# A hybrid decoder block on one core: first tiles regrouped, low weights last, inverse and gates moved by a slot

## The chip, the cores and the metric

One core of a Trainium2 chip runs one launch of the kernel. The metric is the device time in microseconds, the median of several runs. The kernel's engines are TensorE (PE, with its weight loads PEld), VectorE (DVE), ScalarE (ACT), GpSimd (POOL) and SyncE (SP), which issues most of the DMAs.

## What is computed

A residual block over x of 256 tokens by 1024 channels, in float32. From the normalised x come, through one wide projection, a gated DeltaNet branch (8 heads of 128) and a block attention branch (8 heads of 128), each with a SiLU gate; both are projected, merged by sigmoid gates, projected again, normalised and added to x.

```python
h = rms_norm(x, norm_pre_w)
proj = h @ w_in
qkv_a, z_a, beta_a, dec_a, qkv_b, z_b, gate_logits = split(proj)
qkv_a = silu(causal_depthwise_conv(qkv_a, conv_w))           # 4 taps
beta = sigmoid(beta_a)
g = -exp(dn_a_log) * softplus(dec_a + dn_dt_bias)
oa = gated_delta_rule(l2(qa), l2(ka), va, g, beta)          # inverts I + lower
ya = rms_norm(oa, dn_onorm_w) * silu(z_a)
ob = moba_attention(qb, kb, vb, rel_bias)                   # 256 tokens: one causal block, T5 bias
yb = ob * silu(z_b)
merged = gates[0] * (ya @ w_branch[0]) + gates[1] * (yb @ w_branch[1])
out = x + rms_norm(merged @ w_out, norm_post_w)
```

## The kernel before

**Numbers in two parts.** Every large product is made in three products of a rounded type: each operand is split into a high part (a cast to float32r) and a low part (the operand less its high part), and high x high, high x low and low x high are summed in PSUM. For the weights ACT makes w_hi (`split_hi`, L634) and DVE w_lo (`split_lo`, L861), for the normalised, transposed x ACT makes h_hi (L647) and DVE h_lo (L885), for eight chunks k of 128 channels.

**Tiles.** The weights come in 104 tiles of 128 x 1024 values (512 KB), loaded by SP into four slots of `raw` (`load`, L382 to L387): a pair of loads waits on `s_lo`, that is until DVE has made the low part of the tile in the slot. Tiles 0 to 15 are the keys of the eight heads (K) and the attention's values (V) in the order KVKKKVKKKKVVVVVV, tiles 16 to 27 gates, 28 to 75 six tiles for each head, 76 to 79 the last gates, 80 to 95 the branch projections (a hardware loop), 96 to 103 the output projection. One tile is 24 matmuls of 256 columns (`third`, L1236) or, for V, 12 of 512 columns (`value_third`, L1255).

**Slots of the program.** For tiles 0 to 79 each engine's program is written out by one loop over S from 0 to 239: n = S // 3 is the tile, part = S % 3 its third, and TensorE does 8 matmuls (V: 4) in a slot. Every engine works through its slots in order; what an engine does in slot S stands in `gates`, `key_front`, `key_tokens`, `similarity`, `stage_a`, `stage_u`, `stage_w` and so on, each with its own offset. ACT casts tile n + 2 in part 1 and DVE makes its low half in part 2. `stage_u` builds the second half of the triangular inverse of head g from S = U0 + 16 g, with matmuls on TensorE (L1385, L1389, L1393, L1397) and copies and 32 x 32 transposes on DVE; `stage_w` (L1406 and on) uses it from W0 + 16 g.

**The matmuls of a third** go k by k in the order w_hi h_hi, w_hi h_lo, w_lo h_hi, so that the first third already waits for w_lo:

```python
if part == 0:
    pe.wait_ge(s_hi, n + 1)
    pe.wait_ge(s_lo, lo_done(n) if not isinstance(n, int) or n != 1 else 3)
for i in range(8 * part, 8 * part + 8):
    k, which = i // 3, i % 3
```

**The start.** SP loads x in two chunks of 128 tokens. ACT and DVE sum the squares (L637, L639, L867), POOL makes the scales (L450 to L454), ACT scales chunk 0 (L642) and DVE chunk 1 (L874). TensorE runs eight warm-up matmuls (L1195), with the transpose of the small vectors (L1194) after the fifth, then transposes x, both chunks for each k (L1202). ACT casts tile 0's weights between L642 and h_hi; DVE and POOL make half of its w_lo each (L879, L458). Tile 1's w_lo is made in two halves on DVE (L879), then `wbd2`, the low part of the beta and decay weights (L891), for L1212.

**Gates and decays.** The beta and decay products run on TensorE in slot 4 (L1212), 6 and 12 (L1232 to L1234, the cumulative sums), on DVE in slots 5, 7 (L898 to L910), 11 (L916, L919) and 12 (L922 to L926), on ACT in slots 7 and 13, on POOL from L514. POOL then stores the rows of the bias and of the decays and loads them back spread over the partitions (L537 to L546): 1 MB of bias into `xin` (`climbing`), 2 x 512 KB into `th_E` (`E_all`). It copies the bias (L552) and masks the decays (L493), which ACT then takes the exponential of (L674) for `similarity` on DVE (L959). The keys are transposed on TensorE (`key_tokens`, L1316) and read by ACT (L695, L697); each waits for ACT's L697 of the key before.

## Time and profile before

| | us |
|---|---|
| median of 3 runs | 372.43 (372.27 to 372.52) |
| profiled execution | 373.05 |
| its span | 371.3 |
| PE busy | 360.4 (97%) |
| DVE busy | 270.6 (73%) |
| ACT busy | 220.4 (59%) |
| POOL busy | 62.3 (17%) |

The profiled execution is one run of its own, 0.62 us above the median. A busy share tells how long an engine had an instruction under way; matmuls overlap, and the ends of their rows are modelled, so the distance from one start to the next tells the pace. All times of rows are in us from the span's start.

### The profile page before, as it was taken

The page shows a single profiled execution, that of the slowest core. Times are in us where ns is not written, and L with a number is a line of the kernel's source. Part 1 is how long each engine was busy: PE and PEld are TensorE (multiplying, and loading weights), DVE is VectorE, ACT ScalarE, POOL GpSimd, SP SyncE. Part 2 cuts the span into 40 slices and gives each one's busy share as a digit, 9 for nine tenths or more (in the row PEclk, how much of TensorE's full clock was granted, in tenths as well). Part 3 has the DMA queues.
Part 4 walks back from the last instruction along what each step waited for, and adds up shares of the span by engine and source line. Part 5 has one row for each costly group of instructions (what it writes and reads, how often), then busy time and mean ns, then how long its engine had stood idle before and what let it go on. Part 6 is the DMA issues. An engine that isn't in the chain of part 4 may idle for free.

```text
span 371.3 us, 7660 instructions
## 1 busy us (share of the span) xinstructions
PE 360.4 (97%) x2757; PEld 344.9 (93%) x2757; DVE 270.6 (73%) x558; ACT 220.4 (59%) x500; POOL 62.3 (17%) x121
## 2 busy tenths in 40 slices
PE   8999989999999999999999999999999999999993
PEld 5889977899999999999999999999999999999882
DVE  2868886289957778878788678797786557667644
ACT  5777695344455666767757577666676643534531
POOL 3434844520050000202020201002010100000001
PEclk9999999999999999999999999999999999999998
DMA  8658935958698445554556445564446565874633
GB/s 260 178 172 248 321 117 131 286 129 219 162 234 217 127 121 151 151 148 114 140 131 184 117 114 129 146 181 116 113 124 192 140 195 146 220 221 181 229 113 113
DMA packets 99343, 62.45 MB, mean 168 GB/s; under 512 B 3652, under 2 KB 94190, under 8 KB 99310
## 3 DMA queue, kind: packets, MB, share of 16 engines
q1 hardware_dynamic: 98014, 58.59, 57.3%
q0 software_dynamic: 1296, 3.43, 3.1%
q8 instruction: 20, 0.33, 0.4%
q14 instruction: 13, 0.11, 0.1%
HBM read 60.41 MB, written 1.59 MB: 167 GB/s over the span
## 4 chain that ended last, share of the span: by engine, by line
PE 85%; ACT 4%; DVE 4%; DMA 3%; issue 2%; SPq 1%; DVEq 0%; POOL 0%; ACTq 0%; POOLq 0%
PE banks L1251 61%; PE banks L1465 6%; PE banks L1268 4%; DMA raw<-in_w_in_dram 2%; ACT th_E L674 1%; DVE w_lo L861 1%; PE banks L1350 1%; PE banks L1357 1%; ACT w_hi L634 1%; DVE acc L933 1%; ACT h_hi L647 1%; PE banks L1368 1%; DMA y<-in_dn_onorm_w_dram 1%; PE banks L1393 1%; PE banks L1195 1%
## 5 line engine op out<-in xcount | busy, mean ns | idle before, releaser
L1251 PE MATMUL banks<-h_hi,w_hi 128*128 128x256 f32 x576 | 165.6, 287 | 0.3 <-PE banks L1268 0.3
L1251 PE MATMUL banks<-h_lo,w_hi 128*128 128x256 f32 x576 | 165.4, 287 | 0.0
L1251 PE MATMUL banks<-h_hi,w_lo 128*128 128x256 f32 x576 | 165.0, 287 | 0.0
L861 DVE TENSOR_TENSOR w_lo<-raw,w_hi 128x1024 fp32r<-128x1024 f32 x102 | 124.2, 1220 | 33.1 <-ACT w_hi L634 30.2
L634 ACT CAST w_hi<-raw 128x1024 fp32r<-128x1024 f32 x104 | 107.7, 1046 | 9.3 <-PE banks L1465 4.5
L1251 PEld LDWEIGHTS banks<-h_hi,w_hi 128*128 128x128 f32 x576 | 109.9, 191 | 1.5 <-issue 1.3
L1251 PEld LDWEIGHTS banks<-h_hi,w_lo 128*128 128x128 f32 x576 | 110.0, 191 | 0.0
L1251 PEld LDWEIGHTS banks<-h_lo,w_hi 128*128 128x128 f32 x576 | 109.9, 191 | 0.0
L933 DVE SCALAR_TENSOR_TENSOR acc<-banks,vec,acc 128x255 f32<-128x255 f32 (+2 forms) x72 | 34.5, 479 | 6.2 <-ACT acc L730 3.9
L1251 PE MATMUL banks<-y_hi,w_hi 128*128 128x256 f32 x128 | 36.2, 283 | 0.0
L1251 PE MATMUL banks<-y_lo,w_hi 128*128 128x256 f32 x128 | 36.2, 283 | 0.0
L1251 PE MATMUL banks<-y_hi,w_lo 128*128 128x256 f32 x128 | 36.2, 283 | 0.0
L584 POOL TENSOR_TENSOR so<-so,rnq 128x2 f32<-128x2 f32 x8 | 4.4, 554 | 148.2 <-ACT junk L797 148.2
L1251 PEld LDWEIGHTS banks<-y_hi,w_hi 128*128 128x128 f32 x128 | 24.6, 192 | 0.0
L1251 PEld LDWEIGHTS banks<-y_lo,w_hi 128*128 128x128 f32 x128 | 24.6, 192 | 0.0
L1251 PEld LDWEIGHTS banks<-y_hi,w_lo 128*128 128x128 f32 x128 | 24.6, 192 | 0.0
L841 ACT CAST h_hi<-tacc 128x256 f32 x8 | 3.2, 406 | 28.4 <-DVE tacc L1162 28.4
L738 ACT ACTIVATE tz<-banks 128x256 f32<-128x256 f32 x16 | 6.1, 384 | 23.2 <-PE banks L1251 23.1
L730 ACT ACTIVATE acc<-banks,vec 128x256 f32<-128x256 f32 x16 | 7.6, 474 | 15.4 <-PE banks L1251 15.1
L1268 PE MATMUL banks<-w_hi,h_hi 128*128 128x512 f32 x32 | 12.8, 401 | 1.2 <-DVE w_lo L879 0.9
L1268 PE MATMUL banks<-w_lo,h_hi 128*128 128x512 f32 x32 | 12.8, 400 | 0.0
L1268 PE MATMUL banks<-w_hi,h_lo 128*128 128x512 f32 x32 | 12.8, 399 | 0.0
(235 smaller groups left out, 551.0 us busy)
## 6 DMA issues: line engine op xcount, KB each, us to landing
raw<-in_w_in_dram SPq DMA_DIRECT2D x80, 512.0 KB, 5.2
raw<-in_w_branch_dram SPq DMA_DIRECT2D x16, 512.0 KB, 4.9
raw<-in_w_out_dram SPq DMA_DIRECT2D x8, 512.0 KB, 3.7
xin<-in_x_dram SPq DMA_DIRECT2D x2, 512.0 KB, 3.9
xin<-bias_rows POOLq DMA_DIRECT2D x1, 1024.0 KB, 7.6
th_E<-g_rows POOLq DMA_DIRECT2D x2, 512.0 KB, 5.7
raw<-in_x_dram SPq DMA_DIRECT2D x2, 512.0 KB, 4.8
out_dram<-xin SPq DMA_DIRECT2D x4, 256.0 KB, 2.0
```

The source lines that it names most:

```text
L584: pool.tensor_tensor(so[:, 2:4], so[:, 0:2], rnq[:, g % 2, :], ALU.add).then_inc(s_f, 1)
L634: nc.scalar.copy(w_hi[:, t % SLOTS, :], raw[:, t % SLOTS, :]).then_inc(s_hi, 1)
L647: ac(h_hi[:, k, :], bank[k][:, 0:SEQ], ACT.Copy, scale=vec[:, R_PRE + k:R_PRE + k + 1]).then_inc(s_h_hi, 1)
L674: ac(E_all[:, h, c, :], E_all[:, h, c, :], ACT.Exp, bias=ng[:, c, h:h + 1]).then_inc(s_E, 1)
L730: ac(acc[:, t, :], ps, ACT.Copy, scale=tap(CONV - 1, 2 * t, h)).then_inc(s_tap0, 1)
L738: ac(tz[:, t - 4, :], ps, ACT.Tanh, scale=0.5).then_inc(s_tz, 1)
L861: v.tensor_tensor(w_lo[:, t % SLOTS, cols], raw[:, t % SLOTS, cols], w_hi[:, t % SLOTS, cols].bitcast(F32), ALU.subtract).then_inc(s_lo, 1)
L933: v.scalar_tensor_tensor(out=acc[:, a, i:], in0=ps[:, 0:SEQ - i], scalar=tap(CONV - 1 - i, w, h), in1=acc[:, a, i:], op0=ALU.mult, op1=ALU ...
L1195: mm(bank[6][:, 0:SEQ], acc[:, 0, 0:P], acc[:, 0, :], start=True, stop=True)
L1251: last = mm(ps, w, r, start=i == 0, stop=i == 23)
L1268: last = mm(((bE, bF), (bB, bE))[group][c], left, right, start=q == 0 and kk == 0 and which == 0, stop=q == 3 and kk == 1 and which == 2)
L1465: last = mm(bank[2 + 2 * c + e], m[:, k, P * c:P * c + P], w[:, (OUT0 + k) % SLOTS, 512 * e:512 * e + 512], start=k == 0 and m is m_hi and ...
```

## The change

- **Warm-ups:** seven in place of eight; the vector transpose stands after the sixth.
- **Norm of x:** ACT and DVE scale their squares by 1/1024 and DVE adds EPS, so POOL has one operation fewer for chunk 1 (for chunk 0 only the addition of EPS is left in it). ACT scales the second half of chunk 1, DVE the first.
- **Transposes by chunk:** all eight of chunk 0, then all eight of chunk 1 (its k = 4 to 7 wait for ACT's half).
- **Tile 0:** DVE casts w_hi, POOL makes both halves of w_lo; TensorE takes its 24 matmuls in an order written out, each with its own wait.
- **Low weights last:** in every other tile the first third is w_hi h_hi, the second w_hi h_lo, the third w_lo h_hi, and only the third waits for w_lo. V tiles likewise. In the branch tiles the wait for y_lo goes from the third part to the first.
- **Gates:** on DVE from slots 11 and 12 to 9 and 11, on TensorE from 12 to 11, on ACT from 13 to 12.
- **Inverse:** U0 from 100 to 99; the second pair of matmuls and copies at offsets 7, 8, 10, 11 in place of 6, 7, 9, 10, so these keep their slots, and what stands before them goes one slot earlier.
- **POOL:** mask_decay(0) ahead of the bias copy.

```diff
-WARM = 8
+WARM = 7
-U0, W0, UW_STRIDE = 100, 111, 16
+U0, W0, UW_STRIDE = 99, 111, 16
@@ POOL
-                if c == 1:
-                    pool.tensor_tensor(tiny[:, 1:2], tiny[:, 1:2], tiny[:, 4:5], ALU.add).then_inc(s_pre_s, 1)
-                    pool.wait_ge(s_pre_s, 1)
-                pool.tensor_scalar(tiny[:, c:c + 1], tiny[:, c:c + 1], 1.0 / D, EPS, ALU.mult, ALU.add).then_inc(s_pre_r, 1)
+                if c == 0:
+                    pool.tensor_scalar(tiny[:, 0:1], tiny[:, 0:1], 1.0, EPS, ALU.mult, ALU.add).then_inc(s_pre_r, 1)
+                else:
+                    pool.tensor_tensor(tiny[:, 1:2], tiny[:, 1:2], tiny[:, 4:5], ALU.add).then_inc(s_pre_r, 1)
...
-            pool.tensor_tensor(w_lo[:, 0, D // 2:], raw[:, 0, D // 2:], w_hi[:, 0, D // 2:].bitcast(F32),
-                               ALU.subtract).then_inc(s_lo, 1)
-            pool.wait_ge(s_lo, 2)
+            for half in range(2):
+                cols = slice(D // 2 * half, D // 2 * half + D // 2)
+                pool.tensor_tensor(w_lo[:, 0, cols], raw[:, 0, cols], w_hi[:, 0, cols].bitcast(F32),
+                                   ALU.subtract).then_inc(s_lo, 1)
+                pool.wait_ge(s_lo, half + 1)
...
             norms(0)
+            mask_decay(0)
             pool.wait_ge(s_climb, 16)
             pool.tensor_copy(bias[:], climbing[:, :, SEQ - 1::-1]).then_inc(s_bias, 1)
             pool.wait_ge(s_bias, 1)
-            mask_decay(0)
@@ ACT
             ac(xn[:, 0, :], xin[:, 0, :], ACT.Copy, scale=tiny[:, 2:3]).then_inc(s_pre_x[0], 1)
+            sa.wait_ge(s_pre_r, 5)
+            ac(xn[:, 1, D // 2:], xin[:, 1, D // 2:], ACT.Copy, scale=tiny[:, 3:4]).then_inc(s_pre_x[1], 1)
             sa.wait_ge(s_vec, 2)
-            split_hi(0, 0, 1)
...
+            sa.wait_ge(s_hi, 1)
             split_hi(1, 1, 1)
-                elif S == 13:
+                elif S == 12:
@@ DVE
-            v.tensor_scalar(xn[:, 1, :], xin[:, 1, :], tiny[:, 3:4], None, ALU.mult).then_inc(s_pre_x[1], 1)
+            v.tensor_scalar(xn[:, 1, 0:D // 2], xin[:, 1, 0:D // 2], tiny[:, 3:4], None, ALU.mult).then_inc(s_pre_x1a, 1)
+            ve.wait_ge(s_raw[0], 16)
+            v.tensor_copy(w_hi[:, 0, :], raw[:, 0, :]).then_inc(s_hi, 1)
...
-            first_lo(0, 0, s_lo)
-                elif S == 11:
+                elif S == 9:
-                elif S == 12:
+                elif S == 11:
-                elif s == 7:
+                elif s == 8:
-                elif s == 10:
+                elif s == 11:
@@ PE
-                if n == WARM - 3:
+                if n == WARM - 1:
...
-                pe.wait_ge(s_pre_x[c], 1)
-            for k in range(KT):
-                if k == 7:
-                    pe.wait_ge(s_vec, 1)
-                for c in range(NC):
+                pe.wait_ge((s_pre_x[0], s_pre_x1a)[c], 1)
+                for k in range(KT):
+                    if k == 7 and c == 0:
+                        pe.wait_ge(s_vec, 1)
+                    elif k == 4 and c == 1:
+                        pe.wait_ge(s_pre_x[1], 1)
                     last = tp(bank[k][:, P * c:P * c + P], xn[:, c, P * k:P * k + P], ident)
-                last.then_inc(s_hT, 1)
+                    if c == 1:
+                        last.then_inc(s_hT, 1)
-                elif S == 12:
+                elif S == 11:
+            def first_tile():
+                ps = bank[0][:, 0:SEQ]
+                order = ("hh0 hh1 lh0 hh2 lh1 hh3 lh2 hl0 hh4 lh3 hl1 hh5 lh4 hl2 hh6 lh5 hl3 hh7 lh6 lh7 "
+                         "hl4 hl5 hl6 hl7").split()
+                pe.wait_ge(s_hi, 1)
+                pe.wait_ge(s_h_lo, 1)
+                for i, which in enumerate(order):
+                    k = int(which[2])
+                    if which[0] == "l":
+                        pe.wait_ge(s_h_lo, k + 1)
+                    else:
+                        pe.wait_ge(s_h_hi, k + 1)
+                    if which[1] == "l":
+                        pe.wait_ge(s_lo, 1 + k // 4)
...
                 if part == 0:
                     pe.wait_ge(s_hi, n + 1)
-                    pe.wait_ge(s_lo, lo_done(n) if not isinstance(n, int) or n != 1 else 3)
-                elif isinstance(n, int) and n == 1:
-                    pe.wait_ge(s_lo, 4)
-                for i in range(8 * part, 8 * part + 8):
-                    k, which = i // 3, i % 3
...
+                elif part == 2:
+                    pe.wait_ge(s_lo, lo_done(n))
+                for k in range(KT):
+                    w = (w_lo if part == 2 else w_hi)[:, slot, P * k:P * k + P]
+                    r = (right_lo if part == 1 else right_hi)[:, k, :]
+                    last = mm(ps, w, r, start=part == 0 and k == 0, stop=part == 2 and k == KT - 1)
...
-                elif s == 6:
+                elif s == 7:
-                elif s == 9:
+                elif s == 10:
...
-                        if part == 2 and t < 2:
+                        if part == 0 and t < 2:
                             pe.wait_ge((s_ylo_b, s_ylo_a)[t], HEADS)
```

## Rows read from the trace of the kernel before

**Rows 1.** Waits of TensorE, whole span: engine, line, releaser: total us, times, longest.

```profile
PE banks L1316 <- ACT k_all L697: 1.0, 2, 0.6
...
PE banks L1406 <- DVE sub L1100: 0.4, 1, 0.4
```

**Rows 2.** Timeline 0 to 22 us: start, duration, engine, line, operation [idle before <-releaser].

```profile
1.19 4.63 PE L1195 MATMUL banks<-acc 128*128 128x256 f32 x10 [1.19 <-DVE acc L864]
...
6.66 2.78 PE L1195 MATMUL banks<-acc 128*128 128x256 f32 x6
6.74 1.15 ACT L642 ACTIVATE xin<-xin,tiny 128x1024 f32<-128x1024 f32 x1 [0.40 <-POOL tiny L454]
...
7.92 0.75 DVE L874 TENSOR_SCALAR xin<-xin,tiny 128x1024 f32<-128x1024 f32 x1 [0.47 <-POOL tiny L454]
...
9.10 1.71 POOL L458 TENSOR_TENSOR w_lo<-raw,w_hi 128x512 fp32r<-128x512 f32 x1 [1.22 <-ACT w_hi L634]
...
9.90 3.09 ACT L647 ACTIVATE h_hi<-banks,vec 128x256 fp32r<-128x256 f32 x8 [0.94 <-PE banks L1202]
10.41 3.26 DVE L885 SCALAR_TENSOR_TENSOR h_lo<-banks,vec,h_hi 128x256 fp32r<-128x256 f32 x8 [0.72 <-ACT h_hi L647]
...
12.83 1.09 ACT L634 CAST w_hi<-raw 128x1024 fp32r<-128x1024 f32 x1
...
13.97 1.09 ACT L634 CAST w_hi<-raw 128x1024 fp32r<-128x1024 f32 x1
14.03 1.29 DVE L879 TENSOR_TENSOR w_lo<-raw,w_hi 128x512 fp32r<-128x512 f32 x2 [0.36 <-ACT w_hi L634]
...
15.24 0.28 DVE L891 TENSOR_TENSOR wbd<-wbd 128x128 fp32r<-128x128 f32 x1
...
15.47 0.47 PE L1268 MATMUL banks<-w_hi,h_hi 128*128 128x512 f32 x1 [0.89 <-DVE w_lo L879]
...
16.47 0.28 PE L1212 MATMUL banks<-h_hi,wbd 128*32 128x256 f32 x1
```

**Rows 3.** Timeline of TensorE, the transposes of x, in two windows.

```profile
9.44 1.02 PE L1202 MATMUL banks<-cst,xin 128*128 128x128 f32 x4
...
10.29 1.36 PE L1202 MATMUL banks<-cst,xin 128*128 128x128 f32 x11
```

**Rows 4.** Timeline 20 to 30 us, all engines.

```profile
20.79 0.19 DVE L904 TENSOR_TENSOR bd<-banks,bd_lo 128x32 f32<-128x32 f32 x1
...
24.35 1.22 DVE L861 TENSOR_TENSOR w_lo<-raw,w_hi 128x1024 fp32r<-128x1024 f32 x1 [2.50 <-PE banks L1251]
...
27.39 1.23 DVE L861 TENSOR_TENSOR w_lo<-raw,w_hi 128x1024 fp32r<-128x1024 f32 x1
...
27.52 0.60 PE L1232 MATMUL banks<-cst,tab 128*8 128x128 f32 x4
...
28.65 0.99 SPq L387 DMA_DIRECT2D raw<-in_w_in_dram  x2
28.71 0.41 DVE L922 COPY grow<-banks 8x256 f32<-8x256 f32 x1
...
29.96 0.95 POOL L542 DMA_DIRECT2D xin<-bias_rows  x1
```

**Rows 5.** The chain of waits, 35 to 50 us: start, us, what.

```profile
35.29 7.63 DMA raw<-in_w_in_dram
```

**Rows 6.** Timeline of ACT, 42 to 45 us.

```profile
42.95 1.05 ACT L634 CAST w_hi<-raw 128x1024 fp32r<-128x1024 f32 x1 [1.39 <-DMA raw<-in_w_in_dram]
```

**Rows 7.** Busy time by window: window, PE, PEld, DVE, ACT, POOL, PEclk, DMA share, GB/s.

```profile
30.00:32.00 2.00, 2.00 (x17) 1.91 (x16) 1.93 (x4) 1.49 (x3) 0.92 (x1) 1.00 0.98 272
```

**Rows 8.** Timeline of TensorE around L1393 of head 0 and of head 7.

```profile
128.35 0.49 PE L1393 MATMUL banks<-T_all,lac 128*128 128x128 f32 x2
...
271.46 0.49 PE L1393 MATMUL banks<-T_all,lac 128*128 128x128 f32 x2 [0.20 <-DVE T_all L1091]
```

**Rows 9.** Timeline of POOL, 107 to 110 us.

```profile
107.28 2.60 POOL L572 DMA_DIRECT2D T_all<-t_blocks  x4 [3.72 <-DMA t_blocks<-sub]
```

More of the change, by code:

```diff
@@ L1234, in gates, with third @@
                     mm(bA[:, 16:32], ones, tab[:, 9:11, :], start=True, stop=True).then_inc(s_gc_p, 1)
-            def third(n, t, part, right_hi, right_lo, first_tile=False, out_bank=None):
+            def first_tile():
[12 more added lines that the diff above has]
+                        pe.wait_ge(s_lo, 1 + k // 4)
+                    last = mm(ps, (w_lo if which[1] == "l" else w_hi)[:, 0, P * k:P * k + P],
+                              (h_lo if which[0] == "l" else h_hi)[:, k, :], start=i == 0, stop=i == 23)
+                last.then_inc(s_tile, 1)
+            def third(n, t, part, right_hi, right_lo, out_bank=None):
                 ps = bank[t % 2 if out_bank is None else out_bank][:, 0:SEQ]
@@ L1260, in value_third @@
                     pe.wait_ge(s_hi, n + 1)
+                elif part == 2:
                     pe.wait_ge(s_lo, lo_done(n))
-                for m in range(4 * part, 4 * part + 4):
-                    kk, c, which = m // 6, m // 3 % 2, m % 3
-                    if group == 1 and q == 0 and m == 3:
-                        pe.wait_ge(s_vtok, 1)
-                    left = (h_lo if which == 2 else h_hi)[:, 2 * q + kk, P * c:P * c + P]
-                    right = (w_lo if which == 1 else w_hi)[:, slot, 512 * kk:512 * kk + 512]
-                    last = mm(((bE, bF), (bB, bE))[group][c], left, right, start=q == 0 and kk == 0 and which == 0,
-                              stop=q == 3 and kk == 1 and which == 2)
-                    if q == 3 and kk == 1 and which == 2 and c == 0:
-                        last.then_inc(s_vg_p, 1)
+                for kk in range(2):
+                    for c in range(NC):
+                        if group == 1 and q == 0 and part == 0 and kk == 0 and c == 1:
+                            pe.wait_ge(s_vtok, 1)
+                        left = (h_lo if part == 1 else h_hi)[:, 2 * q + kk, P * c:P * c + P]
+                        right = (w_lo if part == 2 else w_hi)[:, slot, 512 * kk:512 * kk + 512]
+                        last = mm(((bE, bF), (bB, bE))[group][c], left, right, start=q == 0 and kk == 0 and part == 0,
+                                  stop=q == 3 and kk == 1 and part == 2)
+                        if q == 3 and kk == 1 and part == 2 and c == 0:
+                            last.then_inc(s_vg_p, 1)
                 if part == 2:
@@ L1448, in _ @@
                         bank_free(n)
-                    third(n, n, part, h_hi, h_lo, first_tile=n == 0,
-                          out_bank=K_TILES.index(n) % 2 if n < GATES_A else None)
+                    third(n, n, part, h_hi, h_lo, out_bank=K_TILES.index(n) % 2 if n < GATES_A else None)
             with pe.Fori(0, KT // 2) as i:
```

18 lines of the change are left out of this document (8 added, 10 removed).

## The prediction

> **What bounds the kernel now.** The profiled execution took 373.05 us (span 371.3); the median of three runs is 372.43, so 0.62 comes off every sum against the profile. I read the page's busy shares first (PE 97% busy), which say only that TensorE sets the time. The second view is what TensorE waited for [rows 1]. It lists hardly 5 us in 371, nearly all in the start; behind it stand 1.0 us in two waits for ACT's L697, 0.4 at L1406, and 0.2 at L1393 [rows 8]. In between, a 256-column matmul starts every 0.12 us, and nothing in the change alters their number. So the time is a start, a fixed queue of matmuls, a few holes and a tail. The change can win only in the start and the holes, and a gain at the start counts only if no hole behind it grows.
>
> The third view is the start in order of time [rows 2]. Eight warm-up matmuls are sixteen records: ten from 1.19, six from 6.66, each 0.43 us. The last holds the queue until 9.23, although x's second chunk is scaled at 7.92 + 0.75 = 8.67. Then ACT makes h_hi (8 in 3.09, from 9.90) and DVE h_lo (8 in 3.26, from 10.41), and ACT casts tile 1 at 12.83. DVE subtracts its low half in two pieces from 14.03 to 15.32, and only then, at 15.47, does TensorE begin tile 1; the beta and decay product (L1212) begins at 16.47. I take that row as the meter of the start.
>
> The fourth view is 20 to 30 us [rows 4]: the decay sums reach DVE at 20.79, then ACT's gates and its cast of tile 4, DVE's low half at 24.35, at 27.39 that of tile 5, which frees the slots for the loads at 28.65. From there [rows 5 to 7]: DVE frees tile 6's slot at 35.29, the load of tile 10 takes 7.63 us because POOL's bias and decay loads share the DMA engines, ACT waits 1.39 us for it and casts at 42.95. ACT is then busy without a break until both of TensorE's waits for L697.
>
> **The start, worked out.** POOL drops one small operation, an estimated 0.3 us, on the way to the second scale, whose user starts at 7.92: it is there at about 7.6. DVE scales half a chunk, less than the 0.75 of the whole, ACT the other half after its first chunk (6.74 + 1.15 = 7.89) by 8.6. Both lie beside the transposes of chunk 0. Six warm-ups ahead of the vector transpose end at 1.19 + 12 x 0.43 = 6.35, where that transpose went anyway (just before 6.66); the seventh ends at 7.52. TensorE idles until 7.9, loads weights and starts the transposes at about 8.1. What follows depends on their pace. The trace has two [rows 3]: 0.21 us start to start until 10.3, and 0.11 after it. The granted clock reads 1.00 (the 2.4 GHz level) in both stretches, so that column doesn't show it; I read the slower cadence as the 1.2 GHz level. TensorE had been stopped from about 5.8 to 6.4 for the vector rows, and was busy from there until the pace doubled. The change fills most of that stop (the queue runs from 1.19 to 7.5 almost unbroken) and opens one of 0.5 us later. At the fast pace chunk 0 takes 0.9, the first h_hi can start at about 9.3 (0.6 earlier); at the slow pace 1.7 and 10.35 (0.45 later). I take the fast one, as the long unbroken stretch now comes first.
>
> DVE's cast of tile 0 has no row of its own. Its bounds are a one-input operation of the same size, 0.75, and the two-input L861, 1.22 [rows 2, 4]; either ends by 9.4, before the first h_lo. POOL then does two halves of 1.71 (before: one), ending near 12.8; the new order asks for the second only behind the last h_lo (about 12.9), so it costs 0, or up to 0.5 if POOL runs slower beside DVE. POOL's memsets move back by as much, into time in which it waits for the gates. ACT no longer casts tile 0 before h_hi, but that cast was hidden.
>
> So h_hi ends near 12.4, ACT's cast of tile 1 near 13.3, DVE's two halves 13.4 to 14.7, L891 14.9. Tile 1 may begin with its high weights alone and isn't the limit; L1212 waits for L891 and starts at 15.1 in place of 16.47: **1.35 earlier** for TensorE. DVE can't follow fully. ACT's cast of tile 2 at 13.97 follows that of tile 1 and its load, which the change doesn't move; I take it as fixed, so DVE's chain through conv comes only 0.4 earlier there, and the decay sums (20.79) by 0.9. Gates on DVE moved from slot 11 to 9 then run behind w_lo of tile 4 (24.35 - 0.9 + 1.22 = 24.7) and end at 25.3. TensorE's gate matmuls, now in slot 11, start at 25.4, before one slot (0.96) later at 27.52. 27.52 - 0.96 - 25.4 = **1.2 is what TensorE carries past the gates**; the hole of about 0.3 ahead of L1232 stays, only smaller or larger with the rest.
>
> **The loads.** The copy of grow (28.71) comes about 2.0 earlier, so POOL's store and its bias load (29.96) go at 27.8. But the gate copies (grow's 0.41 and three small ones, an estimated 0.75 us on DVE) now stand ahead of w_lo of tile 5, which therefore ends at 28.65, as before, and releases the loads of tiles 8 and 9 at the same time as before. The DMA engines begin the saturated stretch [rows 7] about 1.1 earlier with the same bytes; tile 7's low half and the load of tile 10 (35.29) come 0.8 earlier. I put tile 10's landing 1.05 earlier (bounds: 0 and 2.4, where ACT waits no more). ACT is wanted there 1.2 earlier and so waits 1.5 in place of 1.39, and the two holes at L1316 keep their size. **Carried past slot 34: 1.05.** mask_decay(0) ahead of the bias copy is worth nothing here, for ACT reaches the first decay later than the mask even now; the bias copy is 1.5 us later against its use, of which DVE's first similarity has several to spare.
>
> **The rest.** Low weights last: w_lo is due two slots later. After tile 1 no row of TensorE waits for it, so 0. The value tiles signal chunk 0 two matmuls later and ask for the copied bank two earlier, each 0.24 [rows 2]: 0, at worst 0.5 once. The branch tiles ask for all of y_lo a part or two earlier, but its last instruction stands ahead of them in program order: 0. The inverse: its first three steps go one slot earlier, the third and fourth matmul stay. L1393 now has two slots behind DVE's corner transposes. Holes ahead of it [rows 8]: 0.2 idle once, and the stretched 0.49 us rows; start to start I count 0.3 and 0.35 over the usual 0.12. I take 0.55 (bounds 0.2 and 0.7). T_all's load was issued by 109.9 [rows 9], some 10 us ahead of the new first step. L1406's 0.4 stays.
>
> Sum: 1.05 + 0.55 = 1.6. 373.05 - 1.6 = 371.45 profiled; **372.43 - 1.6 = 370.8**, alone 370.2 to 371.4.
>
> **Rivals.** (a) Tile 10 lands early enough, since the decay rows are stored and loaded before the stretch is full: the holes of 1.0 go too, and all of 1.2 is kept: 1.2 + 1.0 to 1.3 + 0.55, about 369.5. For: the store of g_rows now comes before the saturated stretch, so the decay loads are queued early. Against: the same bytes are moved before tile 10's. (b) The slow pace lasts until 10.3: h_hi is 0.45 later, L1212 still 0.5 earlier through tile 1's relaxed wait, DVE's chain not at all; 0.3 + 0.55, so 371.6. (c) The earlier decay loads crowd out tiles 8 to 10, nothing passes slot 34: 0.55, 371.9. (d) The other sign: the slow pace outlasts the transposes by far. Then tile 0's 24 matmuls cost 0.24 each from about 11.0, end at 16.7 in place of 14.4, and push the conv chain that starts from tile 0 by 1.8; 1.5 reach the sums at 20.79, less 0.55 is 373.4. It decides where the pace doubles: past 16 us slower, before 13 no loss. For it speaks the new 0.5 us stop, and that transposes follow it instead of warm-ups; against, that the pace doubled in the middle of transposes before. The Trainium skill (TensorE: Matmul & The Clock Gate, Part 4: PE-mode transpose) says that transposes don't count as busy for the clock; by that rule (d) or (b) is what happens, though the trace, with its doubling among transposes, neither proves nor refutes it. The skill's page DMA: Bandwidth & Descriptors (Queues, rings and completion order) has each DMA engine alternate between queues by packet; by it (c) gains, as POOL's loads get their share whenever they are queued, and the 7.63 us of tile 10's load agrees. (e) Nothing measurable: all is hidden behind tile 10's load.
>
> **How the numbers follow.** Forecast 0.46, (a) 0.16, (b) 0.12, (c) and (e) 0.18, (d) 0.08. A change of 0.2%, 0.75 us, is about what a measurement of this kernel can tell. Faster by more (under 371.68): the forecast, (a), most of (b) and a quarter of the rest, 0.75; within 0.2% 0.17; slower (over 373.18) 0.08. The range leaves out (d) and the far half of (a): 369.5 to 372.2.
>
> **What would show it.** Right: transposes 0.11 apart from about 8.1, h_hi from 9.3, L1212 near 15.1, its gate matmuls near 25.4, the bias load at 27.8, tile 10's cast near 41.9 with a wait of over 1 us, both waits on L697 still there, none on L1393. Wrong: transposes 0.21 apart (b, d); no waits on L697 (a); tile 10 cast after 42.5 (c); new waits in TensorE's list behind 60 us, which I don't have.

## The result and the profile after

The changed kernel takes **374.95 us** (median of four runs, 374.65 to 375.86) beside 372.35 for the kernel before on the same chip: ratio 1.0074, interval 1.0055 to 1.0093. It is slower by 2.6 us, where the forecast was 370.8. The profiled execution took 374.69 us (span 372.9); TensorE's last matmul starts at 366.83 in place of 365.18.

I read it as I read the kernel before: first what TensorE waited for (engine, line, releaser: total us, times, longest), of the changed kernel. L1340 is the old L1316 and L1430 the old L1406, so these lines answer [rows 1].

```profile
PE banks L1340 <- ACT k_all L701: 4.3, 2, 3.9
...
PE banks L1430 <- DVE sub L1105: 0.4, 1, 0.4
```

One wait of 3.9 us is new, and the wait on the inverse (L1393 in [rows 8]) is gone. The start, as a timeline (start, duration, engine, line, operation), of the changed kernel; it answers [rows 2 to 4]:

```profile
7.77 1.97 PE L1208 MATMUL banks<-cst,xin 128*128 128x128 f32 x16 [0.46 <-ACT xin L644]
8.09 0.69 DVE L880 CAST w_hi<-raw 128x1024 fp32r<-128x1024 f32 x1
8.92 2.64 POOL L460 TENSOR_TENSOR w_lo<-raw,w_hi 128x512 fp32r<-128x512 f32 x2 [1.43 <-DVE w_hi L880]
9.08 3.02 ACT L650 ACTIVATE h_hi<-banks,vec 128x256 fp32r<-128x256 f32 x8 [0.75 <-PE banks L1208]
14.70 0.31 PE L1219 MATMUL banks<-h_hi,wbd 128*32 128x256 f32 x1
...
19.19 0.19 DVE L909 TENSOR_TENSOR bd<-banks,bd_lo 128x32 f32<-128x32 f32 x1
...
24.71 0.60 PE L1239 MATMUL banks<-cst,tab 128*8 128x128 f32 x4
```

Everything here came as forecast or earlier: transposes 0.12 us apart, DVE's cast of tile 0 0.69 (bounds 0.75 and 1.22), POOL's halves 1.32 each (taken as 1.71), the first h_hi at 9.1, the meter of the start at 14.70 (forecast 15.1, before 16.47), the decay sums at 19.19, the gate matmuls at 24.7. The loss comes next. The timeline from 26 to 42 us, changed kernel:

```profile
26.58 1.22 DVE L865 TENSOR_TENSOR w_lo<-raw,w_hi 128x1024 fp32r<-128x1024 f32 x1
26.62 0.55 POOL L541 DMA_DIRECT2D g_rows<-grow  x1 [2.64 <-DVE grow L927]
27.16 0.95 POOL L544 DMA_DIRECT2D xin<-bias_rows  x1
...
27.83 1.03 SPq L387 DMA_DIRECT2D raw<-in_w_in_dram  x2
28.55 1.08 POOL L548 DMA_DIRECT2D th_E<-g_rows  x2 [0.43 <-DMA g_rows<-grow]
...
39.05 1.04 ACT L636 CAST w_hi<-raw 128x1024 fp32r<-128x1024 f32 x1 [5.32 <-DMA raw<-in_w_in_dram]
...
41.06 0.66 PE L1340 MATMUL banks<-cst,kT_all 128*128 128x128 f32 x2 [3.91 <-ACT k_all L701]
```

The loads of tiles 8 and 9 are issued at 27.83, earlier than before (28.65), but now POOL's store and bias load stand ahead of them and its decay loads 0.7 us behind. The summaries of the transfers (KB each, median us from issue to landing) for 28 to 31 us of before and 27 to 29 of after:

```profile
raw<-in_w_in_dram SPq DMA_DIRECT2D x2, 512.0 KB, 4.8
xin<-bias_rows POOLq DMA_DIRECT2D x1, 1024.0 KB, 7.6
```

```profile
xin<-bias_rows POOLq DMA_DIRECT2D x1, 1024.0 KB, 7.3
raw<-in_w_in_dram SPq DMA_DIRECT2D x2, 512.0 KB, 11.9
th_E<-g_rows POOLq DMA_DIRECT2D x1, 512.0 KB, 7.4
```

A weight tile that took 4.8 us takes 11.9. ACT, which never waited for tiles 8 and 9 before, waits 5.32, and TensorE behind it 3.91. And the wait has an echo: busy time by window (window, its length, PE busy, PEld, DVE, ACT, POOL, granted clock, DMA share, GB/s) of the changed kernel.

```profile
38.00:41.00 3.00, 0.00 (x0) 0.00 (x0) 0.88 (x1) 1.92 (x7) 2.30 (x2) 0.98 1.11 347
41.00:42.00 1.00, 0.94 (x5) 0.97 (x6) 0.96 (x3) 1.00 (x2) 0.00 (x0) 0.50 0.71 260
42.00:43.00 1.00, 1.00 (x6) 1.00 (x6) 0.96 (x3) 0.23 (x2) 0.00 (x0) 0.50 0.17 49
43.00:44.00 1.00, 1.00 (x6) 1.00 (x6) 1.00 (x1) 0.97 (x6) 0.00 (x0) 0.50 0.00 0
...
45.00:46.00 1.00, 1.00 (x11) 1.00 (x10) 0.60 (x2) 1.00 (x2) 0.84 (x3) 1.00 0.68 96
```

After TensorE has stood still for nearly 4 us its granted clock is 0.50 (the 1.2 GHz level) for about 3 us: 6 matmuls in a microsecond in place of 11. The stretch from the key transposes to the end of the slot's matmuls takes 3.60 us (41.06 to 44.65), and 2.13 in the kernel before, so the clock costs 1.47. For the balance I compare the same matmul in both profiled runs, before and after:

```profile
38.66 0.38 PE L1316 MATMUL banks<-cst,kT_all 128*128 128x128 f32 x2
54.22 0.41 PE L1316 MATMUL banks<-cst,kT_all 128*128 128x128 f32 x2 [0.37 <-ACT k_all L697]
```

```profile
36.03 1.12 PE L1274 MATMUL banks<-h_hi,w_hi 128*128 128x256 f32 x8
57.24 0.41 PE L1340 MATMUL banks<-cst,kT_all 128*128 128x128 f32 x2 [0.37 <-ACT k_all L701]
```

The last of the eight matmuls ahead of the wait starts at 36.87, and at the usual 0.12 the key transposes would have come at 36.99: 1.67 earlier than the 38.66 of before. They come at 41.06, so the hole is 4.07, start to start. With the clock's 1.47 TensorE is then 3.87 later than before. By 57.24 it is 3.02 later, since 0.85 of waits is gone, most of it the old hole at slot 30, and the part with the inverse gains 1.37 up to the last matmul: 4.07 + 1.47 - 1.67 - 0.85 - 1.37 = +1.65, the distance between the last matmuls.

**Why the tile loads are so slow: the packets.** The trace counts packets, bytes and the share of the 16 DMA engines by queue; q1 is SP's, q0 POOL's. First before, 31:32 (tiles 8 and 9 alone) and 34:35 (POOL's loads alone), then after, 34:35, both at once:

```profile
q1 hardware_dynamic: 687, 0.34, 115.0%
...
q0 software_dynamic: 82, 0.34, 99.1%
```

```profile
q0 software_dynamic: 99, 0.36, 87.1%
q1 hardware_dynamic: 99, 0.05, 16.7%
```

0.34 MB in 687 packets is 0.5 KB in each, the row of 128 numbers of a weight tile; 0.34 MB in 82 is 4.1 KB. Once both queues have been moving packets for a microsecond, as many leave one as the other: 54 and 54 at 31:32, 56 and 57, 97 and 100, 99 and 99, 93 and 93 in the microseconds behind it. One for one is then one byte in nine for the weight tiles. While POOL's 2 MB pass (about 512 packets), tiles 8 and 9 get 512 packets of 0.5 KB, a quarter of their 1 MB; the rest takes 2.3 us at 0.33 MB/us, and with POOL's last packets at 36.4 this makes 38.7: ACT's cast starts at 39.05. The Trainium skill (DMA: Bandwidth & Descriptors, Queues, rings and completion order) has each DMA engine take a packet from each queue in turn, and from 31 us on this trace agrees; what the prediction left out is that the turn is blind to size.

**The first microseconds are no turn.** The queue that comes second moves nothing for a while. First after, 29:30 (the tiles issued at 27.83 have no packet until 30.2), then before, 37:38 (tile 10, issued at 35.29, has none until just before 39):

```profile
q0 software_dynamic: 52, 0.21, 84.8%
```

```profile
q0 software_dynamic: 97, 0.36, 99.3%
```

In both microseconds SP's queue has no line. So two things make the 11.9 us: the order of issue (2.4 us without a packet, where tiles 8 and 9 of before had their first 1.0 us behind their issue) and then the packets one for one. What holds the second queue back, no run shows.

The kernel before avoids it by an accident of its order. There the store of g_rows goes behind tiles 8 and 9 and lands 4.6 us later, so the decay loads can't be issued before 34.3; and the bias load, issued at 29.96, 1.3 us behind the tiles, moves nothing until about 33.

### The profile page after: what moved, and what is told of

Read it like the earlier page. It is cut to its first block, busy times and chain, and to the rows that moved or that the text cites. A ratio compares the mean times of both kernels' runs of the same rounds, so it can differ in the third digit from the quotient of the medians.

```text
span 372.9 us, 7655 instructions
## 1 busy us (share of the span) xinstructions
PE 359.8 (96%) x2755; PEld 344.8 (92%) x2755; DVE 268.9 (72%) x558; ACT 219.2 (59%) x500; POOL 62.4 (17%) x121
## 4 chain that ended last, share of the span: by engine, by line
PE 88%; DMA 4%; ACT 4%; DVE 2%; issue 1%; POOL 1%; DVEq 0%; POOLq 0%; ACTq 0%
PE banks L1274 63%; PE banks L1491 6%; PE banks L1292 4%; DMA raw<-in_w_in_dram 3%; ACT th_E L678 1%; PE banks L1374 1%; PE banks L1259 1%; PE banks L1381 1%; PE banks L1392 1%; DMA xin<-in_x_dram 1%; PE banks L1430 1%; PE banks L1219 1%; ACT junk L699 1%; PE banks L1433 1%; PE banks L1437 0%
## 5 line engine op out<-in xcount | busy, mean ns | idle before, releaser
L1274 PE MATMUL banks<-h_lo,w_hi 128*128 128x256 f32 x568 | 83.1, 289 | 0.0
L1274 PE MATMUL banks<-h_hi,w_lo 128*128 128x256 f32 x568 | 82.8, 289 | 0.0
L1274 PE MATMUL banks<-h_hi,w_hi 128*128 128x256 f32 x568 | 82.1, 287 | 0.3 <-PE banks L1292 0.3
L1274 PEld LDWEIGHTS banks<-h_hi,w_hi 128*128 128x128 f32 x568 | 72.7, 191 | 1.4 <-issue 1.4
L1274 PEld LDWEIGHTS banks<-h_lo,w_hi 128*128 128x128 f32 x568 | 73.5, 193 | 0.0
L1274 PEld LDWEIGHTS banks<-h_hi,w_lo 128*128 128x128 f32 x568 | 73.3, 192 | 0.0
L1274 PE MATMUL banks<-y_hi,w_hi 128*128 128x256 f32 x128 | 18.0, 283 | 0.0
L1274 PE MATMUL banks<-y_lo,w_hi 128*128 128x256 f32 x128 | 18.0, 283 | 0.0
L1274 PE MATMUL banks<-y_hi,w_lo 128*128 128x256 f32 x128 | 18.0, 283 | 0.0
L1274 PEld LDWEIGHTS banks<-y_hi,w_hi 128*128 128x128 f32 x128 | 16.5, 192 | 0.0
```

Source lines behind the costliest of these rows:

```text
L1274: last = mm(ps, w, r, start=part == 0 and k == 0, stop=part == 2 and k == KT - 1)
```

## The experiments

All times are medians, each set beside runs of the kernel before on the same chip (372.28 to 372.44). "Version 3" is the kernel of experiment 3, and so on. "Hole" is start to start on TensorE over the usual pace; at slot 30 it is read across the key transposes (from the matmul ahead of them to the one behind, less 0.29), which gives 0.87 for the kernel before. Rows and holes are of one profiled execution of each version.

**1. The gates' slots put back in the change**, all else as changed (the four are ACT's, DVE's two and TensorE's).

```diff
-                elif S == 12:
+                elif S == 13:
...
-                elif S == 9:
+                elif S == 11:
...
-                elif S == 11:
+                elif S == 12:
...
-                elif S == 11:
+                elif S == 12:
```

> The changed kernel with the gate slots as before (DVE 11 and 12, TensorE 12, ACT 13), all else changed. Theory Q (queue order): in the changed kernel POOL's bias load went out at 27.2 us and its decay loads at 28.6, beside the loads of tiles 8 and 9 at 27.8, which then took 11.2 and 12.6 us in place of 4.1 and 5.4. With the gate copies behind the low half of tile 5 again, that low half ends near 26 us and the loads of tiles 8 and 9 are queued 1 us or more ahead of the bias load: they take 4 to 6 us, the hole of 3.8 us ahead of the key transposes and the slow stretch after it are gone, and the time is 370.3 to 371.3. Rival S (the earlier start by itself outruns the loads): the hole stays at 3 us or more, time 374 to 375. Rival M (the mask ahead of the bias copy holds up ACT): no change either, 374 to 375.

Measured: 371.6, ratio 0.9974 (0.9964 to 0.9984). Tiles 8 and 9 are issued at 27.14, the bias load at 28.46, the decay loads at 33.33; the tiles take 5.0 us, the hole of 4 us is gone. A hole of 1.67 at 43.8 is new; experiment 14 explains it.

**2. The gates' slots alone moved in the kernel before** (the same four numbers the other way).

> The kernel before with the gate slots alone moved (DVE 9 and 11, TensorE 11, ACT 12). Theory Q: the bias load comes before the loads of tiles 8 and 9 here too, these take over 9 us, a hole of 2 to 4 us opens ahead of the key transposes at tile 8, and the time is 374 to 377, slower than before. Rival S and rival M: no such hole, for neither the start nor the mask has moved; 372.0 to 372.6.

Measured: 376.94, ratio 1.013 (1.0113 to 1.0147): +4.7 us, with tiles 8 and 9 at 11.7 us and a hole of 3.94 at 41.7. This one part costs more than the change loses; the other parts win some of it back.

**3. The bias load behind the tiles.** In the change POOL waits for conv's eighth tap.

```diff
+            pool.wait_ge(s_tap, 8)
             pool.dma_start(climbing, bass.AP(bias_rows.tensor, 0, ...)).then_inc(s_climb, 16)
```

> The changed kernel with one wait more on POOL: the bias load waits until DVE has done the second conv tap of the third key tile (about 29 us), so it and the decay loads are queued about 1.2 us behind the loads of tiles 8 and 9; the gate slots stay as changed. Theory Q: tiles 8 and 9 land in 4 to 7 us, no hole there, 370.3 to 371.8 (tile 10's load, queued behind the decay rows, may still leave the holes of about 1 us further on). Rival S and M: the hole stays, 374 to 375.

Measured: 370.98, ratio 0.9964 (0.995 to 0.9978). The bias load goes at 29.89 and the decay loads at 30.84, both behind the tiles of 28.08, which take 4.7 us. With 1.8 us between them the order decides (the bias load has its first packets at 32.8, when most of tiles 8 and 9 has passed): one line turns the change from 2.6 us slower to 1.3 faster.

**4. The first mask back behind the bias copy.**

> The changed kernel with the first mask behind the bias copy again. Theory Q and rival S: nothing changes, 374.6 to 375.4, the hole of 3.8 us stays. Rival M: the hole shrinks by 1 us or more and the time falls below 374.

Measured: 374.8, ratio 1.0077 (1.0058 to 1.0096), hole 4.04. The mask's place has no part in the loss.

**5 to 8. Which load starves which, and two other parts.** In 5 the second decay load of version 3 goes behind the first norms; in 6 the change's decay loads wait for tap 12 and the bias load stays early:

```diff
+            pool.wait_ge(s_tap, 12)
             for half in range(2):
```

> The version in which POOL issues its bias load behind the loads of tiles 8 and 9 (370.98), with one more edit: the second of the two decay-row loads is issued after the first norms instead of directly behind the first. Theory Q (a load is served nearly wholly before those queued behind it): tile 10's load, which took 8.2 us and whose cast waited 1.94 us, lands at least 1.5 us earlier, the hole of 1.76 us at slot 30 falls under 0.4, and the time is 369.3 to 369.8. Rival B (the bytes, not their order, bound tile 10's load, since both decay loads share the stretch anyway): 371.0, hole of 1.5 or more. A cost that could appear: the second decay half is wanted by a mask before it lands; then ACT or DVE waits for it and a new hole stands behind slot 34.

> The changed kernel with POOL waiting for the conv taps of tile 7 (about 32 us) before its two decay-row loads; the bias load stays as early as in the change, 27.2 us, ahead of tiles 8 and 9. It tells which of POOL's loads starves tiles 8 and 9. If the decay rows do (queued 0.7 us behind the tiles, so not by order alone): landings of tiles 8 and 9 near 5 us, the hole of 3.8 us gone, 371 to 371.5. If it is the bias load, queued 0.7 us ahead of them: landings stay at 8 us or more, a hole of 2 us or more stays, 373 to 375. I give the bias load 0.6.

Measured: 5 is 370.64 (0.9938 to 0.9971); tile 10's cast waits 0.99 in place of 1.94 and the hole at slot 30 falls from 1.76 to 0.72. The load and the hole moved as the theory has it, the hole by 1.04 of the 1.36 and more that I expected. The median moved by 0.34 from version 3's 370.98, where I expected 1.2 to 1.7, and the two intervals overlap, so a gain in time isn't shown. 6 is 371.83 (0.9979 to 1.0): tiles 8 and 9 take 8.5 us, ACT waits 1.53 for the first and 0.33 for the second, and TensorE doesn't stop for it. My bet was on the bias load, with landings of 8 us or more, which came, and a hole of 2 us or more, which didn't. The bias load costs the tiles 3.7 us and doesn't stop TensorE there; the decay loads beside it cost them another 3.4. Decay loads without an early bias load weren't tried.

7 (version 3, eight warm-ups and the vector transpose three before their end) and 8 (version 3, inverse at the old slots, TensorE's two offsets likewise):

```diff
-WARM = 7
+WARM = 8
...
-                if n == WARM - 1:
+                if n == WARM - 3:
```

```diff
-U0, W0, UW_STRIDE = 99, 111, 16
+U0, W0, UW_STRIDE = 100, 111, 16
...
-                elif s == 8:
+                elif s == 7:
                     ve.wait_ge(s_x_p, 2 * g + 2)
...
-                elif s == 11:
+                elif s == 10:
                     ve.wait_ge(s_d_p, 2 * g + 2)
```

> The version with the later bias load (370.98), with eight warm-up matmuls and the vector transpose three before their end, as in the kernel before. Theory P (the pace of the transposes doubles earlier because TensorE's stop for the vector rows was filled): the transposes of x's first chunk run at 0.21 us again until about 10, h_hi starts 0.5 to 1.0 later, the beta and decay product 0.5 to 1.2 later, and the time is 371.3 to 372. Rival (the pace would have doubled anyway, or the start has room to spare): 371.0, with transposes 0.11 apart.

> The version with the later bias load (370.98), with the first three steps of the inverse at their old slots. Theory: the holes ahead of the inverse's third matmul come back, 0.3 to 0.35 us each, twice: 371.45 to 371.7. Rival: they are taken up by the waits on ACT behind them, 371.0.

Measured: 7 is 370.96, the same as without it; the transposes take 1.97 us from 7.73 there too. So the regrouped warm-ups have no part in the start's gain. 8 is 372.34 (0.9991 to 1.001): +1.36 us in the medians, outside my 371.45 to 371.7. The last matmuls of the profiled runs lie 1.03 apart, but version 8's execution had begun 0.30 earlier; matmul against matmul from 120 us on it falls behind by 1.33. The inverse is worth 2.5 times the 0.55 that I gave it.

**9. The bias load behind the norms, both masks ahead of its copy** (in version 3).

> The version with POOL's loads behind those of tiles 8 and 9 (370.98), with POOL's order changed once more: the two decay-row loads at about 29.8 us, then the first norms, and the bias load (1 MB) only behind these, at about 36.5; both masks come ahead of the bias copy, whose first reader overwrites its source at about 48.5. Theory R, packet by packet: a packet of POOL's queue holds about 4 KB, one of tile 8's or 9's loads 512 B and one of tile 10's 2 KB, and each DMA engine takes one from each queue in turn; so what counts is how many bytes of POOL's are under way beside a tile. Only 1 MB of POOL's (3 us) then stands ahead of tile 10, which lands by 38.5 to 39.5, ahead of ACT's wish (about 40): the hole of 1.76 us at slot 30 falls under 0.3, time 369.2 to 369.8. Rival B, bytes alone (all are moved in the same stretch): 370.6 to 371. What could go wrong: the bias load now crowds out tiles 12 and 13, or its copy is late for the similarity at 48.5, which would show as a new hole of 0.5 us or more behind 45 us.

Measured: 370.68 (0.9928 to 0.9963). My range was 369.2 to 369.8; the time is that of rival B, though tile 10's cast comes at 39.71 and waits for nothing, which speaks against that rival. The hole at slot 30 isn't under 0.3 but 1.94 (in a profiled execution of 371.44, 0.76 above the median, so the median one may have less of it). So a second cause stands behind the first. The timeline of DVE and POOL of this version shows it:

```profile
37.50 3.16 POOL L495 TENSOR_SCALAR_AFFINE_SELECT th_E<-th_E 128x1024 f32<-128x1024 f32 x2
...
43.17 2.07 POOL L557 COPY bias<-xin 128x2048 f32<-128x2048 f32 x1 [2.52 <-DMA xin<-bias_rows]
```

```profile
39.62 1.30 DVE L952 SCALAR_TENSOR_TENSOR kT_all<-tacc,acc 128x256 f32<-128x256 f32 x1
40.85 1.50 DVE L939 SCALAR_TENSOR_TENSOR acc<-banks,vec,acc 128x255 f32<-128x255 f32 x3
...
43.40 2.12 DVE L952 SCALAR_TENSOR_TENSOR kT_all<-tacc,acc 128x256 f32<-128x256 f32 x1
```

kT_all takes 0.42 us where POOL rests. Beside the masks it takes 1.30, beside the bias copy 2.12, and both times it ends 0.3 us behind POOL's instruction (40.92 and 40.66, 45.52 and 45.24). The conv steps of L939, which read a bank and one operand in SBUF, keep their 0.5 us each (three in 1.52 from 36.67, beside the mask). The Trainium skill (SBUF — State Buffer, SBUF: two separate sides) says that DVE and POOL share a pair of ports, and that whichever of a DVE instruction with two SBUF inputs and a POOL instruction that reads SBUF starts first keeps the pair for its whole length while the other stands still; the rows agree, in the time lost and in who loses it.

**10. POOL's loads in pieces of 512 B**, in the change (the bias load likewise).

```diff
-                pool.dma_start(E_flat[:, size * half:size * half + size],
-                               bass.AP(g_rows.tensor, size * half, [[0, P], [1, size]])
-                               ).then_inc((s_E_in, s_E_in2)[half], 16)
+                for b in range(2):
+                    pool.dma_start(E_flat[:, size * half:size * half + size].rearrange("p (a b n) -> p b a n", b=2, n=128)[:, b],
+                                   bass.AP(g_rows.tensor, size * half + 128 * b, [[0, P], [256, size // 256], [1, 128]])
+                                   ).then_inc((s_E_in, s_E_in2)[half], 16)
```

> The changed kernel (374.95) with the bias load and the two decay-row loads each split in two loads whose rows are pieces of 512 B instead of 1 KB and 4 KB; same bytes, same places in POOL's order. If a packet of POOL's queue shrinks with its pieces (512 B), the turn-by-turn rule gives tiles 8 and 9 half of the bytes instead of a ninth: they land 7 to 8 us after their issue in place of 11.2 to 12.6, the hole of 3.8 us falls under 1, and the time is 371 to 372. If POOL's queue packs small pieces into packets of about 4 KB, packets keep their size in the trace, landings stay at 11 us, and the time stays at 375. If instead the queues are served in the order of issue and packets have no part in it, packets shrink but landings stay at 11 us. I give shrinking packets 0.4. POOL's issue time for six loads instead of three could itself delay the decay rows by about 1 us; nothing waits for them there.

Measured: 375.43 (1.0041 to 1.0098), the same as the change. Its packets at 36:37:

```profile
q0 software_dynamic: 99, 0.32, 89.0%
q1 hardware_dynamic: 96, 0.05, 16.2%
```

0.32 MB in 99 packets is 3.2 KB each: POOL's queue packs the pieces. The Trainium skill (DMA: Bandwidth & Descriptors, SWDGE vs HWDGE vs iDMA) has a packet of the software queue hold preferably up to 4096 B, and the trace agrees. Cutting the rows doesn't give the tiles a larger share; it costs POOL's queue 4.85 us of issue for 2.03. It also leaves the size of a packet untried: that the share of bytes follows it is read from the counts, and no run has changed it.

**11. The inverse alone**, in the kernel before.

> The kernel before with the first three steps of the inverse one slot earlier, and nothing else of the change. The prediction gave this part 0.55 us; taking it out of the version with the later bias load cost 1.0 us in the profiled runs and 1.4 in the medians. If it is worth the same on the kernel before: 370.9 to 371.3. If the rest of the difference was something else: 371.6 to 371.9. Either way the two holes ahead of the inverse's third matmul are gone.

Measured: 371.05, ratio 0.996 (0.9945 to 0.9975), -1.39 us. It agrees with experiment 8.

**12. Masks and bias copy in four instructions each**, in version 9.

```diff
+                for h in range(4 * half, 4 * half + 4):
+                    part = E_all[:, h]
+                    pool.affine_select(part, part, [[0, NC], [1, P]], ALU.is_ge, NEG_INF, base=0,
+                                       channel_multiplier=-1).then_inc(s_Em, 1)
+                    pool.wait_ge(s_Em, h + 1)
...
-            pool.tensor_copy(bias[:], climbing[:, :, SEQ - 1::-1]).then_inc(s_bias, 1)
-            pool.wait_ge(s_bias, 1)
+            for q in range(4):
+                pool.tensor_copy(bias[:, 2 * q:2 * q + 2], climbing[:, 2 * q:2 * q + 2, SEQ - 1::-1]).then_inc(s_bias, 1)
+                pool.wait_ge(s_bias, q + 1)
```

> The version with the bias load behind the first norms (370.68; there no load is waited for at slot 30, yet a hole of 1.94 us stays), with each mask in four instructions of one head and the bias copy in four of two heads. Theory D (DVE's instructions with two inputs in SBUF stand still while one of POOL's runs: kT_all took 1.30 and 2.12 us there against 0.42 where POOL rests, the second ending with the bias copy of 2.07 us): such an instruction can now lose 0.5 us at most, DVE's conv for slot 30 starts at 43.5 to 44.2 in place of 45.44, the hole falls to 0.2 to 0.8 and the time to 369.0 to 369.8. Rival: what holds DVE is something else (its own order, PE's banks), kT_all stays over 1.2 us, 370.7.

Its rows of DVE:

```profile
39.53 0.62 DVE L954 SCALAR_TENSOR_TENSOR kT_all<-tacc,acc 128x256 f32<-128x256 f32 x1
...
43.18 1.50 DVE L941 SCALAR_TENSOR_TENSOR acc<-banks,vec,acc 128x255 f32<-128x255 f32 x3
46.88 1.12 DVE L967 SCALAR_TENSOR_TENSOR xin<-banks,tab,th_E 128x128 f32<-128x128 f32 x4 [2.20 <-POOL bias L559]
```

Measured: 370.65 (0.9935 to 0.9968). The mechanism is as expected: kT_all 0.62 in place of 1.30, conv at 43.18 in place of 45.44, hole at slot 30 0.45 in place of 1.94. The time isn't (I expected 369.0 to 369.8): the pieces take POOL longer (5.98 for 3.16, 2.65 for 2.07), the bias copy ends at 46.85, and DVE's first similarity, which writes over the copy's source, waits 2.20 for it; TensorE has new holes of 0.94 and 0.88. That similarity starts at 46.88, as in version 9 (46.87), so what slot 30 wins is lost again there. I put it down to version 9's late bias load and give the pieces to a version that has it early.

**13. The start alone**, with the low weights last that ride with it, in the kernel before.

> The kernel before with the regrouped first steps (and the low weights last, which rode with them), but gate slots, inverse and mask order as before. The beta and decay product is about 1.7 us earlier, as in the change. If what the start wins is lost again by 49 us, because the hole ahead of slot 30 grows by it: 372.0 to 372.5. If part of it passes, as the prediction had it (0.3 to 1.05): 371.2 to 372.0. From the gates-back version (371.6) and the inverse alone (1.4) I reckon the first.

Measured: 371.53 (0.9966 to 0.9988), -0.8 us. My reckoning of 0 from experiments 1 and 11 was wrong: the start keeps 0.8. So the start isn't what experiment 1 lacked.

**14. Start and inverse together**: version 1 with the first mask behind the bias copy. **15.** the same with the copy and the masks in pieces, and ACT waiting for the mask of its own head.

> The gates-back version (371.6: everything of the change but the gate slots) with the first mask behind the bias copy, as in the kernel before; so the kernel before with the regrouped start, the low weights last and the earlier inverse. Theory M2 (the mask ahead of the copy costs where tiles 8 and 9 are in time, because it shifts the bias copy of 2.77 us under DVE's kT_all, which takes 2.11 us there against 0.42 undisturbed): kT_all back at 0.4 to 1.3 us, hole at slot 30 back from 1.67 to about 0.7, and the time is 372.3 - 0.8 (start alone) - 1.4 (inverse alone) = 370.1. Rival: start and inverse don't add (they share a hole), 370.9 to 371.6, with the hole at slot 30 over 1.2.

> The same with the bias copy in four instructions and each mask in four, and ACT waiting for the mask of its own head only. Theory D: kT_all at slot 29 (1.3 us before) takes at most 0.7, DVE's conv for slot 30 comes up to 0.7 earlier, the hole of 0.7 falls to 0.3 or less: 369.6 to 370.0. Rival: the pieces cost POOL 2.7 us more in all (2.65 for 2.07, 5.98 for about 3.2), so the last masks come at 45 us and ACT's decays wait for them; then 370.1 or more and a wait of ACT on th_E.

Measured: 14 is 370.38, ratio 0.9937 (0.9917 to 0.9956); 15 is **369.93**, ratio 0.9923 (0.9903 to 0.9943), with no run above 370.2. The two gains add up (0.8 + 1.4 = 2.2, measured 2.0). Version 14 is version 1 with the first mask behind the copy and nothing else, so the mask's place is worth 371.6 - 370.4 = 1.2 us there, the very edit that the prediction, and experiment 4, had at 0. The rows say how. Version 1 (mask first), then version 14 (copy first):

```profile
38.15 1.10 POOL L495 TENSOR_SCALAR_AFFINE_SELECT th_E<-th_E 128x1024 f32<-128x1024 f32 x1 [1.72 <-DMA th_E<-g_rows]
38.34 1.98 DVE L865 TENSOR_TENSOR w_lo<-raw,w_hi 128x1024 fp32r<-128x1024 f32 x1
39.31 2.77 POOL L555 COPY bias<-xin 128x2048 f32<-128x2048 f32 x1
40.24 2.11 DVE L951 SCALAR_TENSOR_TENSOR kT_all<-tacc,acc 128x256 f32<-128x256 f32 x1
```

```profile
36.46 1.90 POOL L554 COPY bias<-xin 128x2048 f32<-128x2048 f32 x1
38.52 3.18 POOL L495 TENSOR_SCALAR_AFFINE_SELECT th_E<-th_E 128x1024 f32<-128x1024 f32 x2 [0.16 <-POOL bias L554]
39.43 1.32 DVE L951 SCALAR_TENSOR_TENSOR kT_all<-tacc,acc 128x256 f32<-128x256 f32 x1
```

With the mask first, POOL waits for the decay rows before it copies. The mask holds up the low half (1.98 in place of 1.22), the low half the copy (2.77 in place of 1.90), and the copy kT_all (2.11 in place of 0.42). With the copy first it runs beside DVE's conv steps, which it doesn't hold up. In 15 kT_all takes 0.83 (expected 0.7 at most) and the hole at slot 30 is 0.42 (0.73 in 14; expected 0.3 or less). ACT has no wait for a mask, and the time, 0.45 us under 14, is in the expected range.

## Why the prediction was wrong

**The step that failed is "The loads", and with it the term "Carried past slot 34: 1.05".** It saw the pieces: the bias load at 27.8 (it came at 27.16), tiles 8 and 9 at 28.65 (27.83), the store of the decay rows before them. It counted bytes ("about 1.1 earlier with the same bytes") and applied them to tile 10 alone, since tile 10 was the load that ACT waited for in [rows 5, 6]. That POOL's queue would now go ahead of tiles 8 and 9, which nobody had waited for, wasn't priced. Rival (c) named the crowding and the place ("tiles 8 to 10"), but priced it as a gain that doesn't pass, not as a stop: its worst was 0 carried. What came was a stop and a slow stretch of 5.5 us (4.07 + 1.47), and TensorE left slot 30 about 3.0 us later than before in place of 1.05 earlier. Half of the cause can be read in the kernel before: a count of its packets gives 0.5 KB for tiles 8 and 9 and 4.1 for POOL's loads, and with these, one for one, 2 MB of POOL's ahead of the tiles give the 11 us. The other half was misread there. The prediction has tile 10's 7.63 us agree with the turn rule; but tile 10 moved nothing for 3.7 of them, while POOL's packets passed alone, so at first the load issued first had all and not a share.

**The sign.** Rival (d), a slow pace at the start, was the only one that ended slower. It never came: with the new start the transposes ran at 0.12 us (16 in 1.97) and the matmuls behind them at full pace. The Trainium skill (TensorE: Matmul & The Clock Gate, Part 4: PE-mode transpose) has transposes not count as busy; no run here shows a lower clock behind these sixteen, which neither bears the rule out nor refutes it.

**The start**: the order of its steps was right, with POOL's halves (1.32 in place of 1.71) and the product (14.70 in place of 15.1) earlier than worked out. Its size was too small by the profile (1.77 for 1.35) and too large by the medians (0.8 in experiment 13, low weights included). Much of that lies in the profiled execution of before. There the pace doubled at 10.3 us [rows 3]; in experiment 2, which has the same start, the execution's second six warm-up records took 1.47 us and not 2.78, and the beta and decay product began at 15.59 and not at 16.47. In experiment 11, again the same start, it was late (16.74), in a run of 372.34 against a median of 371.05. When the pace doubles differs from execution to execution of the same code. Against 15.59 the new start's 14.7 to 15.0 gains 0.6 to 0.9, which fits the 0.8 of experiment 13; how often the old start has which meter, no run shows. My reason for the fast pace (the filled stop) falls with experiment 7.

**The gates** came at 24.7 where I had 25.4, and their move is what does the harm: copying grow 2.8 us earlier puts POOL's store and bias load in front and its decay loads close behind. The prediction asked what the moved step frees and not which queue it passes.

**Low weights last**: not tried alone. Experiment 13 holds it together with the start, and no row of TensorE waits for w_lo. **The mask**: 0 in the change, 1.2 lost in version 1, without the stop. That the stop hides it is my reading: in the changed kernel both POOL instructions run while DVE waits for tile 8. The prediction looked for who waits for the mask and the copy, and not for whom POOL's instructions hold up. **The inverse**: mechanism right, both holes gone, the term 0.55 measured 1.36 and 1.39. The term counted the holes of heads 0 and 7 alone, each without the second matmul of L1393, which starts 0.21 behind the first where 0.11 is usual. Matmul against matmul, versions 3 and 8 part by 0.41 at head 0, 0.11 at head 1, 0.17 at 171.6 us, 0.18 at head 6 and 0.46 at head 7, together 1.33, and version 11 gains the same 1.33 on the kernel before.

## What to carry to other kernels

Before a step is moved that ends in a DMA, write down what stands in the other queue at its new time, and the packet size of both: here the queue issued first moved alone for 2 to 4 us, and then the packets went in turn, so a queue with packets of 0.5 KB got a ninth of the bytes beside one of 4 KB, and the tile that paid was the next one due, not the one that had waited before. POOL's long instructions had a price on DVE wherever DVE worked from two operands in SBUF; keep them short, or put them where DVE waits or reads a bank. And a meter read from one profiled execution needs a second one of the same code: 0.9 us of this start differed between two executions of it.

## What the runs showed of the hardware

- Once both moved, a queue of 0.5 KB packets and one of 4.1 KB went one for one (99 and 99 in a microsecond), the bytes 0.05 to 0.36 MB. Queues of 2 KB (tile 10's) and 4 KB are less uneven: 67 packets with 0.14 MB and 68 with 0.27 in version 3.
- A load behind a busy queue moved nothing for some time, on either side. POOL's bias load, issued at 27.16 with idle DMA engines, had its first packets at 28.8; issued at 29.89 behind 1 MB of SP's, at 32.8. SP's tiles, issued at 28.65 with idle engines, had theirs at 29.7; issued at 27.83 behind the bias load, at 30.2. So less than 2 us between two issues decided who was starved. Why, stays open.
- POOL's queue packed pieces of 512 B into packets of about 3.2 KB, and a load of half the bytes took POOL about as long to issue or longer: 0.55 us for one of decay rows and 0.95 for the bias, 0.75 and 0.93 for each of their halves.
- After 3.9 us without a matmul TensorE's granted clock stood at 0.50 for about 3 us in the changed kernel, and in experiment 10 from 40 to beyond 46 us. At the start the column reads 1.00 throughout, while the warm-up records go 0.43 us apart and in experiment 2 the second six of them 0.22, so there the cadence has to be read.
- DVE's 0.42 us kT_all took 1.30 and 2.12 us beside POOL's mask and copy, each as one instruction, and 0.62 beside pieces; its steps that read a bank were not touched. It goes both ways: POOL's 1.90 us copy took 2.77 behind DVE's low half (version 1).
